# Position biases of two attention kinds: added by VectorE to the logits in their bank, not accumulated by TensorE

## The reference

```python
# window: 4 heads of 64
dist = jnp.abs(...)                       # query - key
bias = -slopes.reshape(...) * dist        # slopes 2^-1 .. 2^-4
s = jnp.where(allowed, s + bias, NEG_INF) # allowed: dist <= 128
...
# differential: 4 heads of two maps of 32
bias = -slopes[:, None, None] * dist      # slopes 2^-5 .. 2^-8
s = einsum(qi, k) * scale + bias[None, :, None]
p = softmax(s); w = p[:, :, 0] - lam * p[:, :, 1]
```

## Time and profile before

| | us |
|---|---|
| median of 3 runs | 1327.16 (1326.71 to 1328.33) |
| the profiled execution | 1326.52 |
| its span | 1325.2 |
| TensorE busy | 1294.5 |
| VectorE busy | 891.2 |
| ScalarE busy | 757.1 |
| mean granted TensorE clock | 0.998 of full speed |

### The profile page before, as it was taken

How to read it: one execution, slowest core, us unless ns; L and a number is a source line. 1 busy time by engine, 2 the same in 40 slices (tenths; PEclk the granted TensorE clock), 3 DMA queues, 4 the chain that set the end, 5 groups by cost and what they waited for, 6 DMA issues and landing times.

```text
span 1325.2 us, 19473 instructions
## 1 busy us (share of the span) xinstructions
PE 1294.5 (98%) x7715; PEld 1120.3 (85%) x7715; DVE 891.2 (67%) x1299; ACT 757.1 (57%) x1218; POOL 82.5 (6%) x132
## 2 busy tenths in 40 slices
PE   7999999999999999999999999999999999999997
PEld 6888788888888888878888888888888878888886
DVE  5888777776666667667766656656667657766655
ACT  6677665555655555675555555655555575555553
POOL 2121000000000001500000000000000610000000
PEclk9999999999999999999999999999999999999999
DMA  7433686664766655434666664766664434576660
GB/s 242 129 110 131 206 252 208 195 194 129 238 189 187 191 168 145 131 97 143 199 210 189 189 191 148 226 190 190 190 179 129 138 110 149 170 222 191 190 191 32
DMA packets 297292, 228.86 MB, mean 173 GB/s; under 512 B 17631, under 2 KB 273778, under 8 KB 297202
## 3 DMA queue, kind: packets, MB, share of 16 engines
q1 hardware_dynamic: 297186, 227.62, 57.1%
q10 hardware_dynamic: 16, 0.00, 0.0%
HBM read 226.54 MB, written 1.05 MB: 172 GB/s over the span
## 4 chain that ended last, share of the span: by engine, by line
PE 86%; DVE 6%; ACT 5%; issue 2%; POOL 0%; DMA 0%; DVEq 0%; ACTq 0%
PE bank L952 27%; PE bank L955 14%; PE bank L854 10%; PE bank L855 10%; PE bank L856 10%; PE bank L1332 2%; ACT hi_gu L1483 1%; DVE lo_gu L1889 1%; PE bank L918 1%; PE bank L1355 1%; PE bank L924 1%; PE bank L921 1%; PE bank L864 1%; PE bank L1371 1%; ACT hi_dn L1490 1%
## 5 line engine op out<-in xcount | busy, mean ns | idle before, releaser
L952 PE MATMUL bank<-xT,hi_gu 128*128 128x512 f32 x1608 | 400.4, 391 | 0.2 <-DVE lo_gu L1889 0.2
L1889 DVE TENSOR_TENSOR lo_gu<-st_gu,hi_gu 128x2048 fp32r<-128x2048 f32 (+2 forms) x145 | 323.3, 2233 | 88.5 <-ACT hi_gu L1483 88.2
L952 PEld LDWEIGHTS bank<-xT,hi_gu 128*128 128x128 f32 x1608 | 294.8, 188 | 57.0 <-DVE lo_gu L1889 0.4
L1483 ACT ACTIVATE hi_gu<-st_gu 128x2048 fp32r<-128x2048 f32 (+2 forms) x146 | 270.1, 1855 | 25.1 <-PE bank L955 19.9
L955 PEld LDWEIGHTS bank<-xT,lo_gu 128*128 128x128 f32 x1608 | 219.4, 190 | 15.7
L955 PE MATMUL bank<-xT,lo_gu 128*128 128x256 f32 x1608 | 224.2, 282 | 0.0
L854 PE MATMUL bank<-hi_dn,actTh 128*128 128x512 f32 x436 | 171.6, 394 | 2.3 <-DVE actTl L2045 2.3
L855 PE MATMUL bank<-lo_dn,actTh 128*128 128x512 f32 x436 | 170.8, 392 | 0.0
L856 PE MATMUL bank<-hi_dn,actTl 128*128 128x512 f32 x436 | 169.7, 389 | 0.0
L2078 DVE TENSOR_TENSOR act<-act,bank 128x256 f32<-128x256 f32 x101 | 42.5, 421 | 184.4 <-ACT act L1608 184.4
L1490 ACT ACTIVATE hi_dn<-st_dn 128x1024 fp32r<-128x1024 f32 x109 | 113.9, 1054 | 57.2 <-DMA st_dn<-in_ffn_w_down 57.2
(11 more groups left out here) (330 smaller groups left out, 1709.8 us busy)
## 6 DMA issues: line engine op xcount, KB each, us to landing
st_gu<-in_ffn_w_gu SPq DMA_DIRECT2D x176, 512.0 KB, 5.2
st_dn<-in_ffn_w_down SPq DMA_DIRECT2D x109, 512.0 KB, 6.5
st_gu<-in_w_in SPq DMA_DIRECT2D x21, 1024.0 KB, 5.3
st_gu<-in_ffn_w_gate SPq DMA_DIRECT2D x21, 512.0 KB, 4.3
st_gu<-in_ffn_w_val SPq DMA_DIRECT2D x21, 512.0 KB, 5.6
st_gu<-in_w_out SPq DMA_DIRECT2D x16, 512.0 KB, 4.3
st_gu<-in_w_in SPq DMA_DIRECT2D x8, 512.0 KB, 5.1
st_gu<-in_w_out SPq DMA_DIRECT2D x16, 256.0 KB, 4.5
```

Source lines behind the costliest of these rows:

```text
L952: pe.matmul(b[:, :], hv[:, w, k, :], xT[:, k, :, :].rearrange("p a b -> p (a b)"), start=k == 0, stop=k == KD - 1, skip_group_check=True)
L1483: i = act.activation(high, staged, ACT.Copy)
L1889: i = dve.tensor_tensor(low, staged, high.bitcast(F32), ALU.subtract)
```

## The change

The bias matmuls go, and the logit matmuls start their accumulation themselves. In its place VectorE adds the bias ahead of each maximum, reading and writing the bank: two instructions of 128x256 for a win slot (the two heads have different slopes), one of 128x512 for a dif slot (both maps have the same), each followed by a wait of VectorE for itself. The wait for the rounded constants moves with it. The slopes are now constants in the instruction.

```diff
+ALIBI = [float(2.0 ** (-(i + 1))) for i in range(8)]
...
                     if v0 == FIRST_SLOT["win"]:
-                        pe.wait_ge(slopes_ok.sem, slopes_ok["all"])
...
-                    biased = kind in ("win", "dif")
-                    if biased:
-
-                        for v in (v0, v0 + 1):
-                            pr = SLOTS[v][2]
-                            for z in range(2):
-                                pe.matmul(bank[LOGIT_BANK[v]][:, z * S:(z + 1) * S], slopes[:, 2 * pr + z if kind == "win" else 4 + pr, :],
-                                          distances[:, m, 0 if kind == "win" else 1, :], start=(z == 0), stop=False, skip_group_check=True)
...
-                            t = pe.matmul(bank[LOGIT_BANK[v]][:, z * S:(z + 1) * S], q_, k_, start=not biased, stop=True, skip_group_check=biased)
+                            t = pe.matmul(bank[LOGIT_BANK[v]][:, z * S:(z + 1) * S], q_, k_, start=True, stop=True)
...
                     dve.wait_ge(logits_ok.sem, logits_ok[l, v])
+                    logit = bank[LOGIT_BANK[v]]
+                    if v == 0:
+                        dve.wait_ge(slopes_ok.sem, slopes_ok["all"])
+                    if kind == "win":
+                        for z in range(2):
+                            here = logit[:, z * S:(z + 1) * S]
+                            dve.scalar_tensor_tensor(out=here, in0=distances[:, m, 0, :].bitcast(F32), scalar=-ALIBI[2 * pr + z], in1=here,
+                                                     op0=ALU.mult, op1=ALU.add).then_inc(own_v.sem, own_v.one())
+                        own()
+                    elif kind == "dif":
+                        here = logit[:, :].rearrange("p (a b) -> p a b", a=2)
+                        dve.scalar_tensor_tensor(out=here, in0=bc(distances[:, m, 1, :].bitcast(F32), 1, 2), scalar=-ALIBI[4 + pr], in1=here,
+                                                 op0=ALU.mult, op1=ALU.add).then_inc(own_v.sem, own_v.one())
+                        own()
```

## The result

The changed kernel took 1336.09 us (median of four runs, 1332.84 to 1337.38) beside 1327.09 us for the kernel before: a ratio of 1.006, 95% interval 1.0048 to 1.0072. It is slower, as forecast, but by 9 us instead of 2.8, and above the range. The profiled execution is the fastest of the four, 1332.84 us with a span of 1331.5.

A forecast was written before the change was run, and what follows sets the result against it. TensorE, busy 98%, was taken to bound the kernel except where attention's chain leaves it. Each layer's delay grows from +0.32 over +1.15 to +1.4 us; two layers add 2.8 to 1327.16, giving 1330.0 us, range 1327.4 to 1334.0.

The forecast's parts named there:

- The price of an add: VectorE ahead of each maximum, wait for itself included: 0.72 us for a dif slot, 0.79 us for a win slot.
- surcharge of 0.065 us an add: If writing PSUM costs extra access overhead: 0.065 us per added instruction, five a layer on the path, result about 0.7 later.
- Rival 3: Writing the bank is slow: near 1.2 us a dif slot, 1335 to 1337 us, or 1331.0 if milder; chance 0.16.
- first stretch: Layer 0's attention from 532 us to the logits at 550.23: -0.47 for removal, +0.79 for slot 3's adds, +0.32 us.
- GpSimd's work stay as they are: Under what is added: DMAs and GpSimd's work were taken as unchanged by the change, with no cost entered.
- second stretch: Layer 0 from 550 to 591 us, up to unit 9's transposes: delay grows from +0.32 to +1.15 us.
- From 581.86 it is full [...] none of them with idle time ahead: ScalarE after slot 9's maximum, up to the heads' high part at 587.45: no slack, so the +1.04 us delay holds.
- The ring's step from unit 9 to unit 10: Transposes at 590.83 to those at 595.05: less 0.47, plus 0.72 for slot 14's add, +0.25 to 0.27 us.
- only let it wait for ScalarE longer: TensorE before unit 9's transposes: its four savings from removed bias matmuls just lengthen its wait, at no cost.
- TensorE stays the bound: Rival: all 17.8 us added to VectorE hides in its waits and 5.6 us is won, 1321.5 us; chance 0.06.
- partly hidden: Rival: one of four adds on the path has overlooked cover, 0.7 us a layer less, 1328.6 us; chance 0.17.
- The removal gives nothing: Rival: TensorE needs a pause in place of the bias matmuls, losing two times 0.47 a layer, 1331.9 us; chance 0.03.

The follow-up runs named there:

- held remainder: Changed kernel, with VectorE holding its weight remainder for the seventh projection back until GpSimd's rotation of the axial heads is done: 1338.17 us, ratio 1.0074.

## Why the prediction was wrong

**The price of an add** was right: 0.72 and 0.79 us with the wait were worked from 0.69 and 0.42. The adds measured 690 and 420 ns, and from their start to the maximum's it is 0.72 us (582.22 to 582.94) and 0.78 to 0.80 us (538.85 to 539.63, 534.06 to 534.86). The surcharge of 0.065 us an add that the prediction worked out for a write to a bank doesn't show. Rival 3 (a slow write to the bank) is out.

**The path** was right in its sum and, in part, wrong in its makeup. In the first stretch the forecast had +0.32 us and 0.65 came. The step that failed is "GpSimd's work stay as they are": it does the same work, but the earlier VectorE runs into it. Without any adds the stretch is as long, so this part hangs on the removal. The extra 0.33 us are mostly two things, 0.17 and 0.14. VectorE's remainder took 2.74 us instead of 2.57, and by the rows around it the copy of the axial keys could have begun at 550.60; it began at 550.74, since the turn of the keys ahead of it was late, behind GpSimd. In the second stretch +0.83 was forecast and +0.57 came. VectorE and ScalarE in the changed kernel, layer 0, in order of time:

```profile
582.94 0.69 DVE L2310 TENSOR_REDUCE big<-bank 128x2 f32<-128x512 f32 x1
```
```profile
583.67 0.47 ACT L1791 ACTIVATE big<-bank,big 128x256 f32<-128x256 f32 x1 [2.42 <-DVE big L2310]
...
588.98 0.40 ACT L1837 ACTIVATE actTh<-bank 128x256 fp32r<-128x256 f32 x1
```

The maximum of slot 9 is 1.79 us later than in the earlier trace rows, of which 1.08 come from the axial logits: 0.71, as worked out for the add (0.72). ScalarE follows by 1.81. But from there to the heads' high part it takes 588.98 - 583.67 = 5.31 us, before 587.45 - 581.86 = 5.59. "From 581.86 it is full [...] none of them with idle time ahead" was the step: 0.28 us of small gaps stood there, 0.09 ahead of the projection copy and 0.17 ahead of the latent copy, and the later start closes them. The rest to the transposes is 0.12, and 0.11 was forecast. The ring's step from unit 9 to unit 10 is as forecast, +0.26. Altogether 1.48 us a layer against 1.4 (1.56 with the 0.08 us ahead of the ladder). That the sum comes out so near is in part luck: one stretch was 0.33 us too short and the next 0.26 too long. With the clock held up, the changed kernel measures 1329.77 us, where the prediction said 1330.0.

**The clock** is the step that made the forecast fail, and it is worth 6.3 of the 9 us. The forecast carried every TensorE duration over from the profile of before, where the granted clock is 1.00 throughout the attention, and doubled one layer. A longer wait had a cost of zero in it: TensorE's four savings "only let it wait for ScalarE longer", and the growth of the waits before the transposes was named as a sign that the forecast is right. That growth is just what costs: behind it TensorE often does everything at half speed for some microseconds (the eight logit matmuls of layer 1 took 3.58 us instead of 1.89). No rival held it, and the range up to 1334.0 us came from the price of the write, not from this. The Trainium skill ("TensorE: Matmul & The Clock Gate", HAM oscillation — how this bites in real kernels) describes a kernel whose clock falls again and again because of waits between its matmuls. There the waits are for DMAs and last some 3 to 5 us, here they are for VectorE and GpSimd and last 1.0 to 2.0. The runs agree in kind (a granted clock of 0.73 to 0.93 in the windows around such waits), not in length; the section alone would not have named waits as short as these.

**The rivals.** "TensorE stays the bound" is out by the ladder. So is "partly hidden" in the form that it had, one add covered: what the second stretch gave back are 0.28 us of gaps on ScalarE. "The removal gives nothing" was set aside because unbiased groups start without a pause, and this is right for the matmuls themselves (eight logits 1.13 us in both). But its outcome holds in another way: the kernel with no bias at all is not measurably faster than the one before, since in the first stretch its savings go into waits for GpSimd, and some executions have a lower clock besides.

**The signs** announced were right for the VectorE rows, the 4.48 us from unit 9's to unit 10's transposes (4.5 announced), ScalarE's idle time ahead of slot 9's exponentials (1.21 us before, 2.42 after), and the waits before units 9 and 10 (+0.46 and +0.73; about +0.7 announced). The wait before the axial logits was to grow by 0.3 us and shrank from 0.84 to 0.61, because the wait had gone to the axial turn ahead of it.

What stays open: why the same waits let the clock fall in one execution and not in the next, and why one fall costs 1.4 us and another 6.2. The runs give only shares and sizes.

## What to carry to other kernels

Moving work from TensorE to VectorE doesn't end with the sum along the path. If it leaves TensorE with waits that it didn't have before, price them as possible time at the lower clock as well, and look for them above all where the engine is 97% busy and nobody expects an idle clock; matmuls of zeros in such a wait are a cheap test, and here recovered 6.3 of 9 us. And when a change moves VectorE in time without changing GpSimd's work, look at what the two will do at the same moment.

## What the runs showed of the hardware

- The granted clock fell in nine of ten rings in which TensorE waited several times in a row, 1.02 us for unit 9 and then for unit 10 (1.29 us at the upper clock), and in none of ten whose waits ended at 0.77. It fell behind four of eight single waits of 1.9 to 2.0 us, one of two of 1.80, and none of four of 1.17 to 1.61.
- A fall cost from 1.30 us (the changed kernel, layer 1's ring) over 1.50 (its turn) to 6.2 us (held remainder), where the clock stayed down for some 17 us with TensorE busy throughout the last part of it.
- Matmuls of zeros in those waits kept it at 0.998 to 0.999 in eleven of eleven executions. Bias matmuls kept elsewhere, with the waits left open, did not (0.993 to 0.995).
- A GpSimd step of 0.22 us (128x16) lasted 1.20 to 1.26 us while VectorE subtracted two SBUF tensors of 128x1024, and one of 0.39 us (128x96) lasted 1.37. Beside an add that reads a bank and one SBUF tensor it stayed at 0.39. VectorE paid too: the two halves of the remainder took 2.57 us in the kernel before, 2.74 with the collision on the rotation's last step and 2.39 with the hold.
- A VectorE multiply-add in place in a PSUM bank costs what one costs that writes SBUF: 690 ns at 128x512 and 420 at 128x256, beside 682 and 426.
